# Four places of a hybrid decoder step reordered: weight sum before an evacuation, latents' sums inside the last latent item, queries' reciprocal after the keys, y stored by tile pairs

## What is computed

```python
h = rmsnorm(x, ffn_norm[i, 0]);  x = x + 0.5 * swiglu(h, gate, up, down)     # D_FF = 2816
h = rmsnorm(x, mix_norm[i]);     x = x + mixer_i(h)                          # i = 0: latent attention, i = 1: RWKV-7
h = rmsnorm(x, ffn_norm[i, 1]);  x = x + 0.5 * swiglu(h, gate, up, down)
# latent attention, its projections (mla_project and mla_keys)
lat = h @ w_down                                   # 384 query latents, 256 key-value latents, 64 rotary
cq = rmsnorm(lat[..., :384], g_qlat);  c = rmsnorm(lat[..., 384:640], g_kvlat)
kr = apply_rope(lat[..., 640:], cos, sin)
q = rmsnorm(rope_part((cq @ w_uq).reshape(b, l, 8, 192)), g_qn)
k = rmsnorm(concat(c @ w_uk, kr), g_kn)            # eight heads
```

## Time and profile before

| | us |
|---|---|
| runs | 3262.16, 3266.67, 3268.56 |
| median | 3266.67 |
| the profiled execution's own time | 3251.32 |
| its span, first to last instruction | 3249.5 |
| mean granted TensorE clock | 0.965 of full |

### The profile page before, as it was taken

The page is one execution under the profiler, slowest core; times in us unless marked ns, Lnnn a source line. Parts: engine busy times, 40 slices in busy tenths (PEclk is TensorE's granted clock), DMA queues, the critical chain, the costliest instruction groups (busy, mean ns, idle before and its releaser), DMA issues.

```text
span 3249.5 us, 69257 instructions
## 1 busy us (share of the span) xinstructions
PE 3005.7 (92%) x28907; PEld 2865.1 (88%) x28907; DVE 2108.4 (65%) x2688; ACT 1342.4 (41%) x2394; POOL 674.9 (21%) x520
## 2 busy tenths in 40 slices
PE   8999978999999989999999999698788988799998
PEld 8999976679899979999999999678787887799998
DVE  6977844656665663778867788544356554468875
ACT  4433423455555543334433344223345544334432
POOL 1322200310000002113311223100144443212321
PEclk9999988999999999999999999899899999899999
DMA  3222212011111201222222222211000001122222
GB/s 111 101 94 91 78 45 73 23 47 34 34 39 47 73 14 66 78 91 87 91 82 78 91 91 88 98 52 65 17 7 13 17 17 39 65 65 92 89 94 81
DMA packets 77958, 208.10 MB, mean 64 GB/s; under 512 B 25393, under 2 KB 42162, under 8 KB 62578
## 3 DMA queue, kind: packets, MB, share of 16 engines
q1 hardware_dynamic: 77682, 204.16, 19.1%
HBM read 198.63 MB, written 5.49 MB: 63 GB/s over the span
## 4 chain that ended last, share of the span: by engine, by line
PE 71%; DVE 7%; ACT 4%; issue 2%; POOL 1%; POOLq 0%; ACTq 0%; DVEq 0%
PE PS L283 21%; PE PS L438 18%; PE PS L1474 10%; PE PS L2122 6%; PE PS L611 3%; PE PS L1455 1%; PE PS L1501 1%; PE PS L1972 1%; DVE Y L2550 1%; PE PS L1107 1%; PE PS L1108 1%; PE PS L295 1%; PE PS L1126 1%; DVE MXP L1580 1%; PE PS L1478 0%
## 5 line engine op out<-in xcount | busy, mean ns | idle before, releaser
L283 PE MATMUL PS<-XH,WH 128*128 128x288 f32 x1216 | 269.1, 303 | 52.5 <-DVE XL L306 17.9
L267 DVE TENSOR_TENSOR WL<-RAW,WH 128x1536 fp32r<-128x1536 f32 (+3 forms) x112 | 215.1, 1921 | 152.1 <-ACT WH L262 152.1
L262 ACT ACTIVATE WH<-RAW 128x1536 fp32r<-128x1536 f32 (+3 forms) x113 | 173.1, 1533 | 335.5 <-PE PS L283 202.6
L377 POOL TENSOR_TENSOR WLF<-RAW 128x512 f32<-128x512 f32 x72 | 96.2, 1336 | 998.7 <-PE PS L283 661.5
L1474 PE MATMUL PS<-UKMH,CTH 128*128 128x384 f32 (+1 forms) x768 | 271.4, 353 | 6.6 <-issue 5.9
L283 PE MATMUL PS<-XL,WH 128*128 128x288 f32 x1216 | 264.5, 300 | 0.0
L283 PE MATMUL PS<-XH,WL 128*128 128x288 f32 x1216 | 264.3, 300 | 0.0
L438 PE MATMUL PS<-XH,WH 128*128 128x288 f32 x864 | 255.7, 296 | 5.7 <-DVE WL L404 4.0
L1548 DVE TENSOR_REDUCE SS<-SQ 128x4 f32<-128x512 f32 x256 | 173.6, 685 | 128.5 <-ACT SQ L1533 126.6
L438 PE MATMUL PS<-XH,WL 128*128 128x288 f32 x864 | 255.2, 295 | 0.0
L438 PE MATMUL PS<-XL,WH 128*128 128x288 f32 x864 | 254.9, 295 | 0.0
(11 more groups left out here) (541 smaller groups left out, 8541.2 us busy)
## 6 DMA issues: line engine op xcount, KB each, us to landing
RAW<-in_w SPq DMA_DIRECT2D x113, 1024.0 KB, 4.8
RAW<-in_w SPq DMA_DIRECT2D x48, 768.0 KB, 5.0
ROWS<-in_cache_c SPq DMA_DIRECT2D x128, 128.0 KB, 2.0
RAW<-in_w SPq DMA_DIRECT2D x16, 512.0 KB, 4.5
ROWS<-in_cache_kr SPq DMA_DIRECT2D x128, 32.0 KB, 1.8
RAW<-in_w SPq DMA_DIRECT2D x8, 384.0 KB, 3.2
X<-in_x SPq DMA_DIRECT2D x4, 576.0 KB, 7.3
out_y<-X SPq DMA_DIRECT2D x1, 2304.0 KB, 6.9
```

The lines of the kernel that those rows point to most:

```text
L262: act.activation(WH[n % 2][:, 0:cols], RAW[n % 2][:, 0:cols], ACT.Copy).then_inc(rounded, 1)
L267: dve.tensor_tensor(WL[n % 2][:, 0:cols], RAW[n % 2][:, 0:cols], WH[n % 2][:, 0:cols].bitcast(F32), ALU.subtract).then_inc(item_split, 1)
L283: mm = pe.matmul(PS[:, s, 2 * t + half, 0:HT], w[s][:, c:c + P], v[:, k, half * HT:(half + 1) * HT], start=(x == 0 and p == 0), stop=(x == ...
L377: pool.tensor_tensor(sum_place(s, S3, "f"), r(0), r(2), ALU.subtract).then_inc(summed, 1)
```

## The change

In the SwiGLU blocks, `keep_act` waits for four evacuations fewer at the first gate item of a part, and `first_sum_dve` with `first_lo_dve` stand ahead of the evacuation of d = 2. At the start, item 1 is rounded ahead of the last six squares. In the latent stage, the query latents' squares are summed in the middle of the third latent item, their chain (root, reciprocal, three scaled tiles) is put ahead of that item's evacuation, the key-value latents' sums stand ahead of query item 1, their reciprocal behind query item 1 and their tiles behind query items 2 to 4, and the rotary fold ahead of query item 3; the loop over query items is unrolled. In the head stage the queries' reciprocal stands behind the eight key steps. The output is stored by eight transfers, two behind each of the last four down items.

```diff
 keep_act(act, n, js, x, first=False)
-            act.wait_ge(evacuated, n + CREDIT)
+            act.wait_ge(evacuated, n + CREDIT - (4 if first else 0))
 gate_item_act: each keep_act
+        first=x == 0
 plain_act
-        round_item(act, n + x + 1, cols=2 * PLAIN * P if last else ITEM)
+        if n + x:
+            round_item(act, n + x + 1, cols=2 * PLAIN * P if last else ITEM)
 block.scalar, behind xhat_tile of x = 4 to 7 and ahead of square_pair u = 1 to 3
+        round_item(act, 1)
 ffn_dve
-                down_dve(dve, f, d0 + d, d, 4 * len(PARTS) * f + 4 * part + d)
                 if d == 2 and not final:
                     first_sum_dve(dve, d0 + 4, js + cnt, gap=5)
                     first_lo_dve(dve, d0 + 4, js + cnt)
+                down_dve(dve, f, d0 + d, d, 4 * len(PARTS) * f + 4 * part + d)
 lat_pe
-        for u in range(3): ... multiply_item(pe, I_LAT + u, ...)
-        pe.wait_ge(evacuated, I_UQ + CREDIT)
-        pe.wait_ge(lat_sq, 5)
-        (sums of five squares, rotary fold, gains, then wait kr_ok and gains)
-        with pe.Fori(0, H // 2) as pair: ... multiply_item(pe, I_UQ + u, i, QR_T, 2, CQH, CQL, ...)
+        def query_sums(x):
+            if x == 4:
+                pe.wait_ge(evacuated, I_LAT + 2 + CREDIT)
+                pe.wait_ge(lat_sq, QR_T)
+                sums(SQL, QR_T, banks(1, 0))
+        multiply_item(pe, I_LAT + 2, 0, KD, 2, XH, XL, before=query_sums)
...
+        for h in range(H):
+            if h == 1:
+                pe.wait_ge(evacuated, I_UQ + CREDIT)
+                pe.wait_ge(lat_sq, QR_T + KV_T)
+                sums(SQKV, KV_T, banks(0, 2))
+            if h == 3:
+                pe.wait_ge(evacuated, I_UQ + 2 + CREDIT)
+                rope_fold()
+            multiply_item(pe, I_UQ + h, 0, QR_T, 2, CQH, CQL, before=lambda k: pe.wait_ge(lat_split, k + 1),
+                          second={1: lambda: pe.wait_ge(lat_root, 2), 3: folded}.get(h, lambda: None))
 lat_act, behind round_item(act, I_UQ)
+        act.wait_ge(lat_sums, 1)
+        (root of T1); squares(3); latent_hi(0), (1), (2); squares(4)
+        in query item h: h == 0: root of T2; h == 2: copy of KR; h in (3, 4): latent_hi(h) behind the two squares
 lat_dve, behind split_item(dve, I_UQ)
+        dve.wait_ge(lat_root, 1)
+        dve.reciprocal(T1[:], T1[:]).then_inc(lat_rs, 1)
+        latent(0); latent(1); latent_lo(0); latent(2); latent_lo(1); latent_lo(2)
+        evacuate(2)
+        (T3, the rotary tile times TAB)
         for h in range(H):
             split_item(dve, n + 1, ...)
+            if h == 2: wait kr_ok; tensor_copy(GQK[:, 1:2], GAIN_PS[:, 1:2])
             (QN and QR of item h)
+            if h == 1: wait lat_root 2; reciprocal(T2)
+            if h == 2: latent(3); latent(4)
+            if h in (3, 4): latent_lo(h)
 heads_dve
-        dve.wait_ge(q_root, 1)
-        dve.reciprocal(RSQ[:], RSQ[:]).then_inc(q_rs, 1)
         for h in range(H):
             dve.wait_ge(k_mm, h + 1)
             dve.tensor_scalar(KRAW[:, h, 0:SEQ], ...)
+        dve.wait_ge(q_root, 1)
+        dve.reciprocal(RSQ[:], RSQ[:]).then_inc(q_rs, 1)
 block.sync
-        sp.wait_ge(evacuated, N_ITEMS + CREDIT)
-        sp.dma_start(o["y"], X[:]).then_inc(stored, 16)
-        sp.wait_ge(stored, 64)
+        for d in range(4):
+            sp.wait_ge(evacuated, N_ITEMS - 3 + d + CREDIT)
+            for o_ in range(2):
+                sp.dma_start(tiles(o["y"])[:, d, o_, :], tiles(X[:])[:, d, o_, :]).then_inc(stored, 16)
+        sp.wait_ge(stored, 48 + 8 * 16)
```

More of the change, by code:

```diff
@@ L460, in gate_pe, with keep_act @@
         whole(4, again=True).then_inc(multiplied, 1)
-    def keep_act(act, n, js, x):
+    def keep_act(act, n, js, x, first=False):
         act.wait_ge(part_mm, 4 * js + (0, 1, 3)[x] + 1)
@@ L646, in gate_item_act @@
             hidden_act(act, j + x - 1, x - 1)
-        keep_act(act, n + x, js + x, 2)
+        keep_act(act, n + x, js + x, 2, first=x == 0)
         if more:
@@ L931, in lat_sp @@
         load_items(sp, I_UK, 2, 16)
+    KR_PS, GAIN_PS = banks(0, 2), PS[:, 0, 3, HT + 2:HT + 4]
     def lat_pe(pe):
         norm_sums(pe, 1, (I_LAT + 1) % 2)
[L935 to L938, removed]
-        pe.wait_ge(evacuated, I_UQ + CREDIT)
-        pe.wait_ge(lat_sq, 5)
[L941 to L958, removed]
@@ L960, in lat_act @@
-    def lat_act(act):
[L961 to L972, removed]
+        multiply_item(pe, I_LAT, 0, KD, 2, XH, XL, before=lambda k: pe.wait_ge(xhat_split, 8 + k + 1), order=PAIR_ORDER)
@@ new lines, in lat_pe, with sums @@
+        multiply_item(pe, I_LAT + 1, 0, KD, 2, XH, XL, second=lambda: pe.wait_ge(root, 2))
+        def sums(sq, n, out):
+            for half in range(2):
+                for t in range(n):
+                    mm = pe.matmul(out[:, half], ONES, sq[:, t, half * HT:(half + 1) * HT], start=t == 0, stop=t == n - 1)
+            mm.then_inc(lat_sums, 1)
+        def query_sums(x):
[3 more added lines that the diff above has]
+                sums(SQL, QR_T, banks(1, 0))
@@ new lines, in lat_pe, with rope_fold, folded @@
+        multiply_item(pe, I_LAT + 2, 0, KD, 2, XH, XL, before=query_sums)
+        def rope_fold():
+            pe.wait_ge(kr_tab, 1)
+            pe.wait_ge(fold_ok, 2)
+            for half in range(2):
+                pe.matmul(KR_PS[:, half], FOLD2[:], T3[:, half * HT:(half + 1) * HT], start=True, stop=True)
+            pe.wait_ge(gains, 2)
+            pe.matmul(GAIN_PS, FOLD2[:], GQK[:], start=True, stop=True).then_inc(kr_fold, 1)
+        def folded():
+            pe.wait_ge(kr_ok, 1)
+            pe.wait_ge(gains, 4)
@@ L977, in lat_act @@
                 act.activation(CH_[:, t - QR_T, :], KC[:, t - QR_T, :], ACT.Copy).then_inc(lat_hi, 1)
+        norm_root(act, 1, (I_LAT + 1) % 2)
+        round_item(act, I_LAT + 1)
+        squares(0)
+        squares(1)
+        round_item(act, I_LAT + 2)
+        squares(2)
+        round_item(act, I_UQ, cols=6 * P)
+        act.wait_ge(lat_sums, 1)
+        act.activation(halves(T1[:]), banks(1, 0), ACT.Sqrt, bias=vec(V_EPS), scale=1.0 / (QR_T * P)).then_inc(lat_root, 1)
+        squares(3)
+        for t in range(QR_T):
+            latent_hi(t)
+        squares(4)
         for h in range(H):
@@ L980, in lat_act @@
             round_item(act, n + 1, cols=6 * P if h < H - 1 else ITEM)
+            if h == 0:
+                act.wait_ge(lat_sums, 2)
+                act.activation(halves(T2[:]), banks(0, 2), ACT.Sqrt, bias=vec(V_EPS), scale=1.0 / KV).then_inc(lat_root, 1)
+            if h == 2:
+                act.wait_ge(kr_fold, 1)
+                act.activation(halves(KR[:]), KR_PS, ACT.Copy).then_inc(kr_ok, 1)
             act.wait_ge(qn_ok, h + 1)
@@ L984, in lat_act, with evacuate @@
             act.activation(SQR[:, h, :], QR[:, h, :], ACT.Square).then_inc(q_sq, 1)
+            if h in (3, 4):
+                latent_hi(h)
         round_item(act, I_UV)
     def lat_dve(dve):
[L988 to L994, removed]
+        def evacuate(u):
             dve.wait_ge(multiplied, I_LAT + u + 1)
@@ L1024, in lat_dve @@
             dve.tensor_tensor(halves(QR[:, h, :]), banks(n % 2, 2), halves(TAB[:]), ALU.mult).then_inc(evacuated, 1)
+            if h == 1:
+                dve.wait_ge(lat_root, 2)
+                dve.reciprocal(T2[:], T2[:]).then_inc(lat_rs, 1)
+            if h == 2:
+                dve.wait_ge(lat_rs, 2)
+                latent(3)
+                latent(4)
+            if h in (3, 4):
+                latent_lo(h)
         split_item(dve, I_UV)
```

53 lines of the change are left out of this document (38 added, 15 removed).

## The result

| | before | changed |
|---|---|---|
| median of the runs, us | 3266.53 (3262.16 to 3268.56, 4 runs) | 3208.57 (3205.03 to 3214.2, 4 runs) |
| profiled execution, us | 3251.3 | 3205.03 |
| its span, us | 3249.5 | 3203.2 |
| granted TensorE clock, mean | 0.965 | 0.971 |

What follows compares the result with a forecast made beforehand. TensorE, busy 92% of the span, was taken as the bound. Gains of 16.0 + 9.7 + 16.0 + 0 + 3.5 = 45.2 us from 3251.3 gave 3206.1, plus 15.4 carried over 3221.5 us; range 3212 to 3235.

Steps and rivals of the forecast that it cites:

- The median of the runs lies 15.4 above it, and I carry that over: Whole kernel: 15.4 us between profiled execution and median of the runs added to 3206.1, giving 3221.5 us.
- Latent stage, 16.0: Latent stage: 60.8 us become 44.6 plus 0.2 of waiting, a gain of 16.0, ends 11 and 16.5.
- rival 2: Latent stage's query items become bound by the two small engines: 5 us lost, 3226.5 us, chance 0.12.
- Keys, 9.7: Head stage's keys: 21.75 us become 12.0 with the reciprocal behind them, gain 9.7, ends 8.7 and 10.
- The cover of values and key sums: Behind the keys: values (11.3 us) and 32 key-sum matmuls keep TensorE busy during the reciprocals; without it 7.35 returns.
- First gate item, 16.0: SwiGLU blocks, first gate item: waits of 11.1, 4.0 and 1.6 us removed, gain 16.0, ends 6 and 16.7.
- I take 0.2 in each: First gate item: 0.2 us lost in each block to VectorE's waiting behind GpSimd, which could delay M57.
- rival 1: SwiGLU blocks: M57 still late, TensorE waits 2.6 us in all four; gain 6.3, time 3231, chance 0.17.
- Start, 0 with bounds of +0.9 and -1.0: Start: TensorE's 0.85 us wait for item 1's split goes, squares move by 1.0; net 0.
- Store, 3.5: Store of y at the end: two transfers of 288 KB remain after the last evacuation; gain 3.5, ends 2.1 and 4.9.
- rival 3: Store: last two small transfers served one after the other, 5.4 us; gain only 1.5, time 3223.5, chance 0.05.
- Rival 4: Evacuation of d = 2 held up by the weights' load; at a 15 us landing, 3282 us; chance 0.02.

Runs made afterwards that it cites:

- the copy: The kernel before, run once more with no edit: 3258.60 us, ratio 1.0001; its profiled execution has a span of 3261.2 us.
- c2_changed_again: The changed kernel run once more with no edit, on the same chip as the others: 3206.53 us, ratio 0.9863 to the kernel before.
- b1_unroll: The kernel before with only TensorE's loop over the query items written out: 3253.22 us, ratio 0.9984.
- a3_weights: The kernel before with only the weight sum ahead of the evacuation and the kept results' shorter wait: 3243.98 us, ratio 0.9962.

## Why the prediction was wrong

The sign was right; the size was short by 13 us. Against its own baseline the sum looks good, 3206.1 forecast and 3205.0 measured, but that is two sets of errors that cancel.

**"The median of the runs lies 15.4 above it, and I carry that over": this step failed first.** The 15.4 were taken as lying around the program. They were two draws of a stage that scatters: the profiled execution had the shortest recurrence of fourteen, 819.3 us, where the copy of the same program took 834.7, with the clock granted there as the difference; and its runs had a median 7 us above that of 76 later ones. The changed kernel's own profile lies only 3.5 below its median. Without the recurrence, the change is worth 50.9 us by the first two profiles and 47.2 against the copy. So of the 13 us that the forecast of 45.2 lacks against the 58.0 of the medians, 2 to 6 lie in the stages that the sum describes and 7 to 11 in how the recurrence was drawn on the two sides. Against c2_changed_again, whose interval of 37 to 52 us holds the 45.2, the sum could not be told from the measured gain, though the medians (52.9) are 8 apart from it. Whether the changed kernel is granted a better clock in the recurrence is open: 819.8, 823.8 and, with the old start, 829.4 are too few against a spread of 18 us.

**The loop written out is in the diff and in no term of the sum.** It is worth 7.4 to 9.2 us by the stages, 6.2 by b1_unroll's runs. That is more than all that the stages hold beyond the 45.2 (5.7 against before, 2.0 against the copy); without it the sum would have been too high, by what the gate item and the start lost. The row that would have led to it, TensorE waiting 2.9 us for "issue" at 868, was in the trace and is not among the rows that I used.

**Latent stage, 16.0: right.** 16.6 against before, 17.2 against the copy, with no wait and a clock of 1.00 in the third item. The margins that I reckoned as 0 to 0.2 us held; rival 2 did not come.

**Keys, 9.7: right**, 9.2 to 9.3. Eight keys took 12.4 instead of 12.0. The cover of values and key sums held.

**First gate item, 16.0: the term was too large for the changed kernel, 11.8 against before and 12.8 against the copy, and its step on M57 failed.** "I take 0.2 in each" measured 2.06, near rival 1's 2.6. VectorE was freed of 3.47 us there, but the three steps behind the evacuation took 9.25 in all, and 7.06 with the old order (2.92, 1.77 and 2.37): 2.2 came back at once. M57 came 1.24 earlier (108.70 less the later start of 1.14, against 108.80), which is 3.47 less 2.2. TensorE was also there at 106.1 by the times of before (109.30 less 2.06 and 1.14), not at 106.7. Reckoned against the bare times, VectorE lost 4.7 us to GpSimd before and 5.5 after: the waiting was passed on in full, and 0.8 was added. The Trainium skill, page "SBUF — State Buffer", section "SBUF: two separate sides", says that such instructions of VectorE and GpSimd shut each other out; the 4.00 and 1.77 agree with it, and weighing it as a mere bound was too light. Rival 1 then priced its case, 6.3 in all, by waits alone: the gain of 3.2 to 5.8 in each later block holds the half clock that used to stand at the 3.7 us of waiting, and counts for more than the waits' difference of 2.6. In a3_weights, where half clock stands at one M57 wait of four, that brings the gain to 15.9, next to the forecast, and this is luck; in the changed kernel it stands at three of four. In f = 0, where `keep_act` never had the long wait (`if js and x`, with js = 0), the part became 0.3 longer.

**Start, 0 with bounds of +0.9 and -1.0: failed.** It costs 1.1 between the first two profiles and 2.2 to 3.3 against the copy, outside the bound. The squares' move that I had at 1.0 was 0.9; the 1.3 that GpSimd's additions took longer beside the split had no term. I moved the split earlier without asking what runs on GpSimd then.

**Store, 3.5: right**, 4.0. By the rule of the page "DMA: Bandwidth & Descriptors" of the Trainium skill, section "Bandwidth", which asks for batches of a MiB, it would have been rival 3 with 1.5. One transfer of 288 KB took 2.3 us. The fit of the same page, section "Anatomy of one DMA — SWDGE (gpsimd) path", measured there on transfers issued from GpSimd, gave an estimated 2.7. Two transfers, issued one behind the other, ended 3.3 after the last X: at this tail the bytes left to move decided.

Rival 4, the evacuation held up by a load, did not come: no L368 of the changed kernel waits for anything. Its price had a slip: by its own rows the slack is 6.8 and 3.5, 10.3 us, so a landing at 15 us would have cost 56 us and given 3278, not 3282.

## What to carry to other kernels

Before a sum is set against a profiled execution, see whether that execution is a typical one: compare its time with the runs', and where they differ find the stage that varies, because the changed kernel will draw anew. Go through the diff line by line and give each a term, a loop written out too; here a wait for "issue" at a loop's turn marked time that moving the code freed. Work taken from VectorE beside GpSimd's two-input additions came back here as their waiting, 2.2 of 3.47 us, with GpSimd's work left as it was. And where a wait of 3.7 us of TensorE was removed, the half clock that stood at it came back as well, unless the wait that took its place, 2.1 us, brought it again.

## What the runs showed of the hardware that I had not expected

- The same recurrence, with waits of 121.5 to 124.6 us, takes 819 to 837 us from one execution to the next; 40 us windows have a granted clock of 1.00 in one and 0.93 to 0.95 in the other.
- TensorE stands for 2.6 to 3.2 us at the turn of a loop, waiting for nothing that the trace shows to be late, and then works at half clock; the two turns cost 3.4 to 4.6 us each. 24 matmuls put in front of unrelated code 370 us earlier take 5.4 us of that away.
- A step moved out of GpSimd's shadow runs at its bare 0.68 us, and its neighbour takes over the waiting: 4.00 us for two steps of 0.91.
